# The second block's attention: its 16 heads taken in pairs instead of one by one

## The reference

```python
sc = jnp.einsum('bqkgd,bskd->bkgqs', qblk, k) * scale      # group A: heads 0 to 7
p = jax.nn.softmax(sc, axis=-1)
o = jnp.einsum('bkgqs,bskd->bqkgd', p, v)
...
sc = sc - slope * dist                                      # group B: heads 8 to 15
sc = jnp.where(valid, sc, NEG_INF)
m = jnp.maximum(sc.max(-1), sink_l)
p = jnp.exp(sc - m[..., None])
denom = p.sum(-1) + jnp.exp(sink_l - m)
o = jnp.einsum('bkgqs,bskd->bqkgd', p / denom, vb)
...
oa, ob = rms_norm_2(oa, gn_a_g), rms_norm_2(ob, gn_b_g)
mix = jnp.concatenate([oa, ob], axis=-1) @ w_o[l]
h = layer_norm(DEEPNORM_ALPHA * h + mix, ln1_g[l], ln1_b[l])
```

## Time and profile before

| | us |
|---|---|
| runs before: median (lowest to highest of 3) | 2533.08 (2533.03 to 2535.03) |
| the profiled execution: its own time | 2531.32 |
| its span from first to last instruction | 2529.5 |
| PE busy in the span | 2457.2 (97%) |
| DVE, ACT, POOL busy | 1723.4, 1252.5, 537.4 |
| one attention stretch, first score matmul to the turn of group B's output | 70.76 (layer 0), 70.76 (layer 1) |

### The profile page before, as it was taken

The page is one execution under the profiler, slowest core; times in us unless marked ns, Lnnn a source line. Parts: engine busy times, 40 slices in busy tenths (PEclk is TensorE's granted clock), DMA queues, the critical chain, the costliest instruction groups (busy, mean ns, idle before and its releaser), DMA issues.

```text
span 2529.5 us, 43732 instructions
## 1 busy us (share of the span) xinstructions
PE 2457.2 (97%) x17339; PEld 2228.4 (88%) x17339; DVE 1723.4 (68%) x3045; ACT 1252.5 (50%) x2676; POOL 537.4 (21%) x423
## 2 busy tenths in 40 slices
PE   7899999999999999999999999999999999999997
PEld 6768998998789999999888878789999999888885
DVE  4647345445669777888777556759876888777555
ACT  5442235444555554444555555555454444555553
POOL 3601144455258400000000002458500000000000
PEclk9999999999999999999999999999999999999998
DMA  5400045654245565555787665335665555777664
GB/s 175 141 9 26 18 143 182 189 182 148 82 126 169 182 189 182 180 184 181 228 245 236 192 206 158 101 109 167 185 183 184 180 185 180 224 239 239 194 206 126
DMA packets 148074, 421.07 MB, mean 166 GB/s; under 512 B 15904, under 2 KB 49056, under 8 KB 147488
## 3 DMA queue, kind: packets, MB, share of 16 engines
q1 hardware_dynamic: 144080, 405.34, 52.1%
q0 software_dynamic: 2192, 8.99, 1.0%
q10 hardware_dynamic: 1600, 3.96, 0.4%
HBM read 400.40 MB, written 17.83 MB: 165 GB/s over the span
## 4 chain that ended last, share of the span: by engine, by line
PE 90%; DVE 6%; ACT 2%; DMA 1%; issue 0%; POOL 0%; DVEq 0%; ACTq 0%; SPq 0%
PE pb L429 89%; PE pb L438 1%; DVE arena L1563 1%; ACT arena L1110 1%; DVE arena L1566 1%; DMA raw<-in_vT 1%; ACT L1110 0%; DVE arena L1713 0%; DMA H<-in_x 0%; DVE arena L1645 0%; ACT hi L1098 0%; DVE arena L1622 0%; DVE H L1563 0%; DVE sm L1885 0%; DVE arena L2015 0%
## 5 line engine op out<-in xcount | busy, mean ns | idle before, releaser
L1098 ACT CAST hi<-raw 128x512 fp32r<-128x512 f32 x1402 | 814.5, 620 | 387.2 <-PE pb L429 177.7
L429 PE MATMUL pb<-HTh,hi 128*128 128x256 f32 (+1 forms) x2968 | 857.6, 289 | 0.2
L429 PE MATMUL pb<-HTl,hi 128*128 128x256 f32 (+1 forms) x2968 | 842.4, 284 | 0.0
L429 PE MATMUL pb<-HTh,lo 128*128 128x256 f32 (+1 forms) x2968 | 841.6, 284 | 0.0
L2294 POOL TENSOR_TENSOR lo<-raw,hi 128x512 fp32r<-128x512 f32 x383 | 516.6, 1372 | 595.6 <-ACT hi L1098 595.2
L1573 DVE TENSOR_TENSOR lo<-raw,hi 128x1024 fp32r<-128x1024 f32 x464 | 565.5, 1219 | 83.9 <-ACT hi L1098 83.9
L429 PEld LDWEIGHTS pb<-HTh,hi 128*128 128x128 f32 x2968 | 569.9, 192 | 2.7 <-DVE arena L1563 0.7
L429 PEld LDWEIGHTS pb<-HTl,hi 128*128 128x128 f32 x2968 | 570.5, 192 | 0.9
L429 PEld LDWEIGHTS pb<-HTh,lo 128*128 128x128 f32 x2968 | 569.7, 192 | 0.0
L429 PE MATMUL pb<-hi,WH 128*128 128x512 f32 x1112 | 434.2, 391 | 7.9 <-DVE WL L2258 7.8
L429 PE MATMUL pb<-lo,WH 128*128 128x512 f32 x1112 | 433.6, 390 | 0.0
(11 more groups left out here) (194 smaller groups left out, 2268.1 us busy)
## 6 DMA issues: line engine op xcount, KB each, us to landing
raw<-in_uT SPq DMA_DIRECT2D x256, 512.0 KB, 3.7
raw<-in_vT SPq DMA_DIRECT2D x256, 512.0 KB, 4.2
raw<-in_w_ffn_in SPq DMA_DIRECT2D x44, 512.0 KB, 3.9
raw<-in_wq SPq DMA_DIRECT2D x32, 512.0 KB, 3.6
wk<-kept SPq DMA_DIRECT2D x128, 128.0 KB, 4.4
raw<-in_w_in SPq DMA_DIRECT2D x24, 512.0 KB, 3.8
raw<-in_w_ffn_out SPq DMA_DIRECT2D x22, 512.0 KB, 4.4
raw<-in_w_gate SPq DMA_DIRECT2D x16, 512.0 KB, 3.5
```

What stands on the lines that cost most here:

```text
L429: return e.matmul(o, l, r, start=start, stop=stop)
L1098: e.copy(u.hi[k], u.half[k]).then_inc(*s.up("hi", ("hi", g)))
```

## The change

The loop over 18 steps becomes one over eight pairs `p`. `HEADS` sets the order: a pair holds a head of each key head, so 0 with 4, 1 with 5, and so on. Below, "place" is the position `n` in `HEADS`. The scores of a pair are issued as four matmuls that alternate between its heads, into banks 0 and 1, after both banks are free. Iteration `p` then turns the two heads of pair `p - 1` and takes the values of pair `p - 2`. `warm` stays in pairs 3 to 7 alone, with six matmuls each.

Iteration 0 holds both projection units instead. The five tiles are turned together in iteration 2, into banks 4 and 5, and copied by ACT behind pair 2's exponentials. `PT` gets a fourth buffer; DVE makes the copies of places 0 to 5, ACT those of 6 to 15. The four gain steps move from DVE to POOL. The root of group A's norm moves behind the last exponential, the norm itself behind all maxima, and group A's four output chunks and all four output units behind that, around the last values.

```diff
+HEADS = [0, 4, 1, 5, 2, 6, 3, 7, 8, 12, 9, 13, 10, 14, 11, 15]
+TILES = (9, 5, 6, 7, 8)
...
-        self.PT = [ar(13824 + i * 512, 512) for i in range(3)]
+        self.PT = [ar(13824 + i * 512, 512) for i in range(3)] + [ar(0, 512)]
...
-FOUR, OA, OBT = (0, 1, 2, 3), (3, 2), (2, 3, 4, 5)
+FOUR, OA, OBT = (0, 1, 2, 3), (0, 1), (2, 3, 4, 5)
...
+        def at_scores(n):
+
+            pair = HEADS[n:n + 2]
+            for b, h in enumerate(pair):
+                f = 5 * (h // 8)
+                emptied(b)
+                w.wait_ge(*s.to("qt", l, f + h % 4))
+                w.wait_ge(*s.to("qt", l, f + 4))
             for t in range(2):
-                x = mm(PB[b][:, t * 256:(t + 1) * 256], m.QT[r, f + j, t * 128:(t + 1) * 128], m.QT[r, f + 4, :], True, True)
-            x.then_inc(*s.up("score_ps", ("score_ps", l, h)))
-            free[b] = [("nmx", l, h)] if g else [("px", l, h)]
-
-        def at_turn(h):
-            i, b = h % 3, 2 + h % 2
+                for b, h in enumerate(pair):
+                    r, f = PAR[h % 8 // 4], 5 * (h // 8)
+                    x = mm(PB[b][:, t * 256:(t + 1) * 256], m.QT[r, f + h % 4, t * 128:(t + 1) * 128], m.QT[r, f + 4, :], True, True)
+                    if t:
+                        x.then_inc(*s.up("score_ps", ("score_ps", l, h)))
+                        free[b] = [("nmx" if h > 7 else "px", l, h)]
+
+        def at_turn(n):
+            h, i, b = HEADS[n], n % 3, 2 + n % 2
...
-        def at_pv(h):
-            i, g, hh = h % 3, h // 8, h % 8
+        def at_pv(n):
+            h, i = HEADS[n], n % 4
+            g, hh = h // 8, h % 8
...
-        for h in range(18):
-            if h < 16:
-                at_scores(h)
-            if h < 2:
-                project(2, 2 + h, 4)
-            if 5 <= h < 10:
-                turn_tile((9, 5, 6, 7, 8)[h - 5], 2 + h % 2, ("qb", l))
-            if h in (15, 16):
-                turn_out("oa", [h - 15], OA)
-            if 1 <= h <= 16:
-                at_turn(h - 1)
-                if h > 2:
-                    warm((h - 1) % 2, 5)
-            if h == 17:
-                out_product(0)
-            if h >= 2:
-                at_pv(h - 2)
+        for p in range(8):
+            at_scores(2 * p)
+            if p == 0:
+                project(2, 2, 4)
+                project(2, 3, 4)
+            else:
+                at_turn(2 * p - 2)
+                at_turn(2 * p - 1)
+            if p == 2:
+                for k, f in enumerate(TILES):
+                    turn_tile(f, 4 + k % 2, ("qb", l))
+            if p > 1:
+                at_pv(2 * p - 4)
+                at_pv(2 * p - 3)
+            if p > 2:
+                warm(4 if p < 6 else 6, 6)
+        at_turn(14)
+        at_turn(15)
+        at_pv(12)
+        at_pv(13)
+        turn_out("oa", (0, 1), OA)
+        at_pv(14)
+        at_pv(15)
         turn_out("oa", (2, 3), OA)
+        out_product(0)
         for n in (1, 2, 3):
             out_product(n)
         turn_out("ob", range(4, 8), OBT)
...
-                if h > 2:
-                    w.wait_ge(*s.to("pt_ps", l, h - 3))
+                if n > 2:
+                    w.wait_ge(*s.to("pt_ps", l, HEADS[n - 3]))
...
-        for h in range(18):
-            if h == 2:
+        def weights(n):
+
+            w.wait_ge(*s.to("pt_ps", l, HEADS[n]))
+            w.wait_ge(*s.to("pv_ps", l, HEADS[n - 4]))
+            e.copy(m.PT[n % 4], PB[2 + n % 2][:, :]).then_inc(*s.up("soft", ("pt", l, HEADS[n])))
+
+        for p in range(8):
+            at_scores(2 * p)
+            at_scores(2 * p + 1)
+            if p == 0:
+                take("win", l, 2, 2)
+                take("win", l, 2, 3)
+            elif p == 1:
                 second_group()
-            elif h == 9:
+            elif p == 2:
+                for k, f in enumerate(TILES):
+                    w.wait_ge(*s.to("qt_ps", l, f))
+                    e.copy(m.QT[:, f, :], PB[4 + k % 2][:, 0:256]).then_inc(*s.up("qkv2", ("qt", l, f)))
+            elif p == 3:
                 split_high(units.i + 3)
-            elif h == 13:
-                w.wait_ge(*s.to("o_ms", l, 0))
-                fn(m.s16[:, :, 0:8], m.v16[:, :, 0:8], ACT.Sqrt).then_inc(*s.up("roots", ("o_root", l, 0)))
-            if h < 16:
-                at_scores(h)
-            if h < 2:
-                take("win", l, 2, 2 + h)
-            if 9 <= h <= 16:
-                w.wait_ge(*s.to("pt_ps", l, h - 1))
-                w.wait_ge(*s.to("pv_ps", l, h - 4))
-                e.copy(m.PT[(h - 1) % 3], PB[2 + (h - 1) % 2][:, :]).then_inc(*s.up("soft", ("pt", l, h - 1)))
-            if h in (15, 16):
-                turned(("oa", l), [h - 15], OA, f"gn{l}")
-            if h == 15:
+            elif p == 7:
                 w.wait_ge(*s.to("sinks", l))
                 fn(m.snk[:, 8:16, :], m.snk[:, 8:16, :], ACT.Exp).then_inc(*s.up("soft", ("snk", l)))
+            if p > 3:
+                weights(2 * p - 2)
+                weights(2 * p - 1)
+        w.wait_ge(*s.to("o_ms", l, 0))
+        fn(m.s16[:, :, 0:8], m.v16[:, :, 0:8], ACT.Sqrt).then_inc(*s.up("roots", ("o_root", l, 0)))
+        weights(14)
+        weights(15)
+        turned(("oa", l), (0, 1), OA, f"gn{l}")
         turned(("oa", l), (2, 3), OA, f"gn{l}")
...
+                w.wait_ge(*s.to("px", l, HEADS[n - 3]))
...
-        for h in range(18):
-            if h < 16:
-                at_scores(h)
-            if 5 <= h < 10:
-                turn_tile((9, 5, 6, 7, 8)[h - 5], 2 + h % 2)
-            if 1 <= h <= 8:
-                w.wait_ge(*s.to("pt_ps", l, h - 1))
-                e.tensor_copy(m.PT[(h - 1) % 3], PB[2 + (h - 1) % 2][:, :]).then_inc(*up("tiles", ("pt", l, h - 1)))
-            if 4 <= h <= 7:
-                gain_step(h - 4, ("in", l), m.BC2 if l else m.bc, 2 * l)
-            if h == 10:
+        for p in range(8):
+            at_scores(2 * p)
+            at_scores(2 * p + 1)
+            if 1 <= p <= 3:
+                for n in (2 * p - 2, 2 * p - 1):
+                    w.wait_ge(*s.to("pt_ps", l, HEADS[n]))
+                    e.tensor_copy(m.PT[n % 4], PB[2 + n % 2][:, :]).then_inc(*up("tiles", ("pt", l, HEADS[n])))
+            elif p == 5:
                 over(0)
                 values(0, 0)
-            elif h == 11:
                 values(0, 1)
-            elif h == 12:
+            elif p == 6:
                 head_mean(0, 0)
                 head_mean(0, 1)
-            elif h == 13:
-                head_root(0)
-                head_norm(0, 0)
-            elif h == 14:
-                head_norm(0, 1)
-            elif h == 15:
+            elif p == 7:
                 own()
                 sink = m.bcs[:, o + 128:o + 136].unsqueeze(2).to_broadcast([128, 8, 2])
                 tt(m.snk[:, 8:16, :], m.nmx[:, 8:16, :], sink, A).then_inc(*up("scores", ("sinks", l)))
-            if h in (15, 16):
-                turned(("oa", l), [h - 15], OA, f"gn{l}")
+        head_root(0)
+        head_norm(0, 0)
+        head_norm(0, 1)
+        turned(("oa", l), (0, 1), OA, f"gn{l}")
         over(1)
...
+        bc = m.BC2 if l else m.bc
+        w.wait_ge(*s.to("bc", 2 * l))
+        for t in range(2):
+            tt(m.Hv[:, t, :], m.Hv[:, t, :], bc[:, 0:1024], M).then_inc(*s.up("gains_pool", ("gain", ("in", l), t)))
+        for t in range(2):
+            w.wait_ge(*s.to("gain", ("in", l), t))
+            tt(m.Hv[:, t, :], m.Hv[:, t, :], bc[:, 1024:2048], A).then_inc(*s.up("gains_pool", ("gained", ("in", l), t)))
         split_low(units.i + 3)
```

More of the change, by code:

```diff
@@ L2004, in vector, with at_scores @@
         ts(m.sk8, m.bcs[:, o + 128:o + 136], 8.0, None, M).then_inc(*up("scores"))
-        def at_scores(h):
-            g, hh, b, i = h // 8, h % 8, h % 2, h % 3
+        def at_scores(n):
+            h = HEADS[n]
+            g, hh, b, i = h // 8, h % 8, n % 2, n % 3
             src = PB[b][:, :]
```

11 lines of the change are left out of this document (3 added, 8 removed).

## The result

The changed kernel takes 2538.98 us (median of 8 runs, 2534.94 to 2545.42), the kernel before 2532.63 (8 runs, 2525.71 to 2536.45). The ratio of the means is 1.0034, with an interval of 1.0021 to 1.0046: the change makes the kernel 8.6 us slower (the medians alone differ by 6.4). The forecast was 3.4 us faster; the time lies in the range, 2521 to 2549, and on the other side of no change.

What follows compares the result with a forecast made beforehand. The attention loop was taken to be bound by PE's list of work and waits. Per layer -16.8 + 9.9 + 2.2 (port) + 3.0 (clock) = -1.7 us, -3.4 for both: 2529.7 us, range 2521 to 2549.

Steps and rivals of the forecast that it cites:

- Work taken from PE: Attention loop: fewer `warm` matmuls, scores of a pair overlapping, old waits gone; PE's list 16.8 us shorter a layer.
- New waits: Attention loop: PE waits at four new places, 2.4 + 2.5 + 2.2 + 2.8 = 9.9 us a layer.
- (1): Between scores of pairs 1 and 2: PE waits 2.4 us until pair 1's exponentials free both score banks.
- (2): At the tiles: the third waits 2.3 us for ACT's copy of the first, the last two 0.2 more.
- (3): Group B: PE's turns wait 0.45 and 0.1 us in each pair, 2.2 over four pairs.
- (4): Loop end: PE waits 1.8 us ahead of place 14's turn and 1.0 ahead of the turn of group A's output.
- The port: Pairs 1 and 2: POOL's SBUF operations delay DVE's two-input operations; 2.2 us a layer, bounds 0.5 and 3.8.
- The clock: Around pair 2 and the tiles: quiet PE drops to half clock; 3.0 us a layer, bounds 0.5 and 12.
- rival R2: The clock falls and stays low until the output product: some 3.8 us per further pair, slower; chance 0.26.
- Rival R3: Scores of a pair do not overlap: each pair 1.0 us more, +8 a layer, 2545; chance 0.05.
- structure: Attention loop without port and clock: the terms -16.8 us of PE work and old waits, +9.9 of new waits, a layer.
- The forecast's own case: Whole kernel: port between 0.5 and 3.8 us, clock between 0.5 and 5, spanning 2522 to 2537; chance 0.53.

Runs made afterwards that it cites:

- the one in pieces: The changed kernel with each gain step on POOL cut into four pieces of 128 x 256, 16 operations in a row: 2542.38 us.
- the fastest version: Changed kernel, gains on DVE (last two ahead of group B's output turn), pair 0's values before the tiles, second projection unit in pair 1, end filled: 2505.72 us.

## Why the prediction was wrong

**Work taken from PE: right.** A pair's scores take 1.13 us (forecast 1.2), `warm` costs 0.11 each, the old waits are gone. The stretch without port and clock is 64.3 us against 63.9 worked out, and the kernel with all waits filled is 12.6 us faster than before, against 13.8. (The 0.6 us that pair 1's two negations lose beside the `lo` parts is in that.)

**New waits: right.** (1) 2.4 and some tenths of port: 2.91. (2) 2.3 and 0.2: 2.08 and 0.19 once the port is out. (3) 2.2 over group B: 0.48, 0.37, 0.37, 0.58 and 0.37 in layer 0 of the changed kernel, 2.17. (4) 1.8 and 1.0: 1.76 and 0.97.

**The port: the step that failed.** The term was 2.2 us a layer, at most 3.8, and rested on "pair 2's first loses between 0 and 2.0, its second up to 1.3, since POOL starts again while DVE reduces". It measured 6.4 us a layer (12.9 for both; 10.4 by the other order). The picture behind the term, that DVE is let in at the end of the POOL operation it meets, came from rows of the kernel before, and it is what the chip does when the DMAs don't stand ahead: 1.38 + 1.47 and 0.43 + 1.47 us. The two DMAs stood in the order of POOL's list, just ahead of the four steps, and I read them only as DMAs that keep their place. I gave the case no rival: a hold to the end of the row, 7 us, would have been one, and it could have been priced from the row's 8 us (9.3 measured).

The Trainium skill's rule (SBUF — State Buffer, section "Who interferes with whom"), that the blocked side waits for the whole of the other's instruction, agrees with the kernel that has its DMAs behind the row, and is too mild for the changed one, where the wait spans three or four instructions, and for the one in pieces, where it spans twelve. The same section has tensor_scalar among the operations that can contend and tensor_reduce as one that never does; L1589 at 2.28 us and L2043 at 0.69 beside POOL agree.

**The clock: right in kind, a little low.** 6.0 us was forecast for both layers, 8.3 measured (3.5 at the first two waits, 4.8 at the end), each with 4 to 5 us of uncertainty. The spell came where it was expected, in the waits (1) and (2), and was over before pair 4's scores in both layers (674.4 against 677.4, 1640.3 against 1643.1), so rival R2 didn't happen. A second spell, over the last values and the first output unit, was in the forecast only as "a further one is possible".

**Rival R3** is out (1.13 us a pair), and its price of 8 a layer was too high: 3.3 measured, since waits absorbed the rest, where the text said next to nothing.

Sum for both layers: structure off by 1.2 us, port by 8.5, clock by 2.3, together the 12.0 us between -3.4 and +8.6. The sign hung on the port. With its term as forecast the other measured terms come to +0.1, and the kernel with the DMAs behind the row, where the port costs about what was forecast, measured -2.5 (-5.1 to -0.3). The small gain that was forecast is hardly told from no change. That 2539 lies in the stated range is luck: its upper part was there for R2, a clock that does not come back, and the port filled it. (The forecast's own case, 2522 to 2537, begins at 2521.3 by its terms.)

## What to carry to other kernels

When a row of operations goes to POOL, look at what stands just ahead of it in POOL's list: after DMAs that POOL issues itself, a row without a gap kept DVE out to its end or nearly (6 to 10 us here), where behind other work it cost at most one operation at a time. Put the DMAs behind the row, leave a gap, or keep the row away from DVE operations with a short way to PE. The first two were tried here, on rows of four operations. And fill a long wait of PE with work of the list (8 us here for values ahead of the tiles), else with matmuls on constants (6 us).

## What the runs showed of the hardware

- POOL's two DMA issues followed by a row of SBUF operations: DVE held 5.9 to 10.2 us, in all twelve meetings (two layers of six kernels), to the end of the row or one piece short of it. Without the DMAs just ahead, all fifteen meetings with the row (seven with the DMAs 20 us earlier, eight in two profiles with them behind) ended at the next end of a POOL operation.
- In one case an operation that began 0.2 us after the first DMA's issue, 0.9 us ahead of the row, was already held. In the changed kernel the hold outlasted the DMAs' landing (663.9 against 660.4).
- A `TENSOR_SCALAR` of 128 x 2 with one SBUF input was held like one with two (2.28 us instead of 0.17 with the DMAs long before, 10.18 with them just ahead), a `TENSOR_REDUCE` from SBUF beside the same row was not (0.69).
- In the other direction, DVE's two steps of 1.2 us took 3.45 us beside POOL's `lo` parts (1.22 and 2.32), and eight of these 12.02 instead of 10.07, of which the first two, beside the steps, took 2.29 and 2.25 instead of 1.3.
- Two heads' score matmuls on different halves of the array's rows: 1.13 us for eight records; on the same half 1.99.
- The scatter between executions was 19 us (2519.1 to 2538.1, 12 runs) with the gains on DVE, 9 us with all waits filled and 6 us in the fastest version (6 runs each). The spells alone don't explain it: it was 7 us (12 runs) with the DMAs behind the row, where each layer has a spell of some 17 us.
